# A recurrence's half-array products ordered head by head or in turn, and a slab begun on half its tokens

## What is computed

```python
# recurrence, per head
S_t = S_{t-1} diag(w_t) - (S_{t-1} kk_t)(kk_t*a_t)^T + v_t k_t^T ; y_t = S_t r_t
# the two borders
x = x + _rms_norm(mixed, norm_mix_post[i])
h = _rms_norm(x, norm_ffn_pre[i])                       # first border, then h @ w_ffn_up
f = jnp.square(jax.nn.relu(h @ w_ffn_up[i])) @ w_ffn_down[i]
x = x + _rms_norm(f, norm_ffn_post[i])
h = rmsnorm(x, norm_mix_g[l])                           # second border, then h @ w_in
```

## Time and profile before

| | us |
|---|---|
| median of three runs | 1532.68 (1531.84 to 1535.1) |
| the profiled execution | 1532.59 |
| its span, first to last instruction | 1530.8 |
| TensorE matmul busy | 1437.6 (94%) |
| VectorE busy | 736.2 (48%) |
| ScalarE busy | 613.0 (40%) |
| GpSimd busy | 473.7 (31%) |

### The profile page before, as it was taken

How to read it: one execution, slowest core, us unless ns; L and a number is a source line. 1 busy time by engine, 2 the same in 40 slices (tenths; PEclk the granted TensorE clock), 3 DMA queues, 4 the chain that set the end, 5 groups by cost and what they waited for, 6 DMA issues and landing times.

```text
span 1530.8 us, 19427 instructions
## 1 busy us (share of the span) xinstructions
PE 1437.6 (94%) x7762; PEld 1146.2 (75%) x7762; DVE 736.2 (48%) x1176; ACT 613.0 (40%) x960; POOL 473.7 (31%) x172
## 2 busy tenths in 40 slices
PE   6999999899889999999997999999999989699997
PEld 5878877688667888888886888777887867577763
DVE  3355367733354541514215199336353245566664
ACT  4443345322352432323214234654434444365552
POOL 2452023000124664645532454422233520200001
PEclk9999999657898999999998999999999999799998
DMA  6232123000134444444443234211223602889964
GB/s 215 90 117 70 32 88 110 2 1 1 42 138 132 157 136 153 140 149 143 146 150 111 83 108 126 83 55 35 105 83 137 214 11 103 341 333 422 412 270 180
DMA packets 98815, 207.61 MB, mean 136 GB/s; under 512 B 6785, under 2 KB 56321, under 8 KB 92065
## 3 DMA queue, kind: packets, MB, share of 16 engines
q1 hardware_dynamic: 91808, 181.13, 34.5%
q10 hardware_dynamic: 4608, 16.78, 2.8%
q0 software_dynamic: 2304, 8.39, 1.5%
HBM read 170.63 MB, written 35.65 MB: 135 GB/s over the span
## 4 chain that ended last, share of the span: by engine, by line
PE 82%; DVE 6%; ACT 5%; issue 3%; DMA 3%; POOL 1%; SPq 0%; POOLq 0%; DVEq 0%; ACTq 0%
PE bank L517 22%; PE bank L499 13%; PE bank L501 13%; PE bank L500 12%; PE bank L2876 4%; PE bank L809 3%; PE bank L785 3%; PE bank L800 2%; PE bank L1206 2%; ACT whi L428 1%; PE bank L706 1%; PE bank L2813 1%; PE bank L1160 1%; PE bank L1265 1%; PE bank L1280 1%
## 5 line engine op out<-in xcount | busy, mean ns | idle before, releaser
L436 POOL TENSOR_TENSOR wlo<-raw,whi 128x2048 fp32r<-128x2048 f32 (+2 forms) x83 | 378.7, 4562 | 652.7 <-ACT whi L428 616.4
L428 ACT ACTIVATE whi<-raw 128x2048 fp32r<-128x2048 f32 (+1 forms) x84 | 159.1, 1894 | 274.7 <-PE bank L501 267.4
L517 PE MATMUL bank<-alo,whi 128*128 128x512 f32 x368 | 149.2, 406 | 5.0 <-DVE alo L728 5.0
L2005 DVE TENSOR_TENSOR ffn_relu<-ffn_relu 128x512 f32<-128x512 f32 x32 | 97.6, 3051 | 106.7 <-ACT ffn_relu L1985 106.7
L517 PE MATMUL bank<-ahi,whi 128*128 128x512 f32 x368 | 146.5, 398 | 0.0
L499 PE MATMUL bank<-alo,whi 128*128 128x512 f32 (+1 forms) x360 | 141.5, 393 | 0.0
L501 PE MATMUL bank<-ahi,wlo 128*128 128x512 f32 (+1 forms) x360 | 140.3, 390 | 0.0
L500 PE MATMUL bank<-ahi,whi 128*128 128x512 f32 (+1 forms) x360 | 140.1, 389 | 0.0
L517 PE MATMUL bank<-ahi,wlo 128*128 128x512 f32 x368 | 91.7, 391 | 0.0
L517 PEld LDWEIGHTS bank<-alo,whi 128*128 128x128 f32 x368 | 71.3, 194 | 23.5 <-DVE alo L728 6.2
L517 PEld LDWEIGHTS bank<-ahi,whi 128*128 128x128 f32 x368 | 71.2, 193 | 15.5 <-issue 0.7
(11 more groups left out here) (517 smaller groups left out, 2994.0 us busy)
## 6 DMA issues: line engine op xcount, KB each, us to landing
raw<-in_w_in_dram SPq DMA_DIRECT2D x18, 1024.0 KB, 5.3
expert_gate_up<-in_expert_w_gate_dram SPq DMA_DIRECT2D x17, 1024.0 KB, 11.2
expert_gate_up<-in_expert_w_up_dram SPq DMA_DIRECT2D x17, 1024.0 KB, 13.9
expert_down<-in_expert_w_down_dram SPq DMA_DIRECT2D x17, 1024.0 KB, 8.7
raw<-in_w_ffn_up_dram SPq DMA_DIRECT2D x16, 1024.0 KB, 6.2
raw<-in_w_ffn_down_dram SPq DMA_DIRECT2D x16, 1024.0 KB, 5.6
raw<-in_w_in_first_dram SPq DMA_DIRECT2D x12, 1024.0 KB, 5.3
expert_rows_dram<-zero_rows SPq DMA_DIRECT2D x23, 512.0 KB, 6.9
```

Source lines behind the costliest of these rows:

```text
L428: nc.scalar.activation(whi[:, n % SPLIT, 0:k * c], raw[:, n % RAW, 0:k * c], ACT.Copy).then_inc(hi_made, 1)
L436: nc.gpsimd.tensor_tensor(wlo[:, n % SPLIT, 0:k * c], raw[:, n % RAW, 0:k * c], whi[:, n % SPLIT, 0:k * c].bitcast(F32), ALU.subtract).the ...
L517: ins = nc.tensor.matmul(acc, of, by, start=first and i == 0, stop=last and i == products - 1)
L2005: nc.vector.tensor_tensor(relu2[:, n % 2, :], relu[:, n % 2, :], relu[:, n % 2, :], ALU.mult).then_inc(up_sq, 1)
```

## The change

In the recurrence, the products of the two heads alternate in the masks, q, g, h and y. A mask stage now fills one bank for each head at the same time, and VectorE stores the masks in the new order. At both borders the function `pe_wide_early` does the first slab's 32 products with `whi` on the first 256 tokens before the last tiles are there: those of the first unit after the third turn, those of the second after the fourth. The 32 products on the last 256 tokens and the 16 with `wlo` on all 512 follow behind `columns_ready`. At the second border, ScalarE's and VectorE's lists have the second tile's split earlier.

```diff
+        def pe_wide_early(pe, name, turned):
...
+            for unit, cs in units:
+                pe.wait_ge(hi_made, n + 1)
+                pe.wait_ge(cols_lo, turns[turned]["split"] + NT // 2 * turns[turned]["halves"])
+                accs[unit] = banks.open(pe, unit)
+                for i in range(k):
+                    nc.tensor.matmul(accs[unit][:, near], wh[:, i, cs], alo[:, i, near], start=i == 0, stop=False, skip_group_check=True)
+                    nc.tensor.matmul(accs[unit][:, near], wh[:, i, cs], ahi[:, i, near], start=False, stop=False, skip_group_check=True)
+                yield
+            columns_ready(pe, turned)
+            for unit, cs in units:
+                for i in range(k):
+                    for acts in (alo, ahi):
+                        nc.tensor.matmul(accs[unit][:, far], wh[:, i, cs], acts[:, i, far], start=False, stop=False, skip_group_check=True)
+            pe.wait_ge(lo_made, n + 1)
+            for unit, cs in units:
+                for i in range(k):
+                    ins = nc.tensor.matmul(accs[unit][:, :], wl[:, i, cs], ahi[:, i, :], start=False, stop=i == k - 1, skip_group_check=True)
+                banks.filled(ins, unit)
+            yield
...
-            in_turn(turn)
+            in_order("turn early turn early early", turn=turn, early=early)
...
+            in_halves = [(NCH * h + c, h, c) for c in range(NCH) for h in range(2)]
...
-            for i, (src, h, c) in enumerate((src, h, c) for src in (b.beta, b.khat) for h in range(2) for c in (0, 2)):
-                acc = banks.open(pe, f"{u}mask{i}")
+            for i, (src, c) in enumerate((src, c) for src in (b.beta, b.khat) for c in (0, 2)):
+                names = [f"{u}mask{2 * i + h}" for h in range(2)]
+                accs = [banks.open(pe, name) for name in names]
                 for j in range(2):
...
+                    for h in range(2):
+                        ins = nc.tensor.matmul(accs[h][:, j * 256:(j + 1) * 256], src[half(h), (c + j) * CHUNK:(c + j + 1) * CHUNK],
+                                               b.kr[half(h), c + j, :, :].rearrange("p a n -> p (a n)"), start=True, stop=True)
...
-            for n, (h, c) in enumerate(units):
+            for n, h, c in in_halves:
...
+            for c in range(NCH):
+                cs = slice(c * CHUNK, (c + 1) * CHUNK)
+                for h in range(2):
+                    nc.tensor.matmul(yacc[half(h), cs], b.neg_w[:, NCH * h + c, 0:HD], b.ab[:, 1, NCH * h + c, :], start=c == 0, stop=False,
+                                     skip_group_check=True)
+                for h in range(2):
+                    nc.tensor.matmul(yacc[half(h), cs], b.vtok[:, c, half(h)], b.bd[:, 1, NCH * h + c, :], start=False, stop=True,
+                                     skip_group_check=True)
...
-            in_order("post norm post norm split post norm post slab norm split split split",
+            in_order("post norm post norm split post split norm post slab norm split split",
                      post=act_fed(act), norm=act_norm(act, "mix2", lambda t: x[:, t, :], x_ready_after(2), scratch3, sums3),
...
-            in_order("out gained post out gained norm post norm out gained post out gained norm post split norm split split split",
+            in_order("out gained post out gained norm post norm out gained post out gained norm post split split norm split split",
                      out=dve_last_down(dve), gained=dve_fed(dve), post=dve_post(dve, 1), split=dve_split(dve, "mix2", ahi, alo),
...
-            columns_ready(pe, "mix2")
-            for n in ("glu_gate0", "glu_gate1", "glu_a0", "glu_a1", "fq0", "fq1", "fk0", "fk1"):
+            for n in ("glu_gate1", "glu_a0", "glu_a1", "fq0", "fq1", "fk0", "fk1"):
```

More of the change, by code:

```diff
@@ L586, in pe_rows_open, with pe_rows_close @@
                 yield
-        def pe_rows_close(pe, names, units, turn, **how):
+        def pe_wide_early(pe, name, turned):
+            n = slab_no[name]
+            k, c = slab_shape(n)
+            wh, wl = view(whi, n % SPLIT, k, c), view(wlo, n % SPLIT, k, c)
+            near, far = slice(0, T // 2), slice(T // 2, T)
+            units = [(f"{name}/{j}", slice(j * P, (j + 1) * P)) for j in range(c // P)]
+            accs = {}
+            for unit, cs in units:
[17 more added lines that the diff above has]
+            yield
+        def pe_rows_close(pe, names, units, turn, early, **how):
             for t, hf in ((0, 0), (1, 0), (0, 1), (1, 1), (2, 0), (2, 1), (3, 0), (3, 1)):
@@ L1202, in pe_rwkv @@
             st.after("pool", "r")
-            for i, (src, h, c) in enumerate((src, h, c) for src in (b.beta, b.khat) for h in range(2) for c in (0, 2)):
-                acc = banks.open(pe, f"{u}mask{i}")
+            for i, (src, c) in enumerate((src, c) for src in (b.beta, b.khat) for c in (0, 2)):
+                names = [f"{u}mask{2 * i + h}" for h in range(2)]
+                accs = [banks.open(pe, name) for name in names]
                 for j in range(2):
[L1206 to L1210, removed]
+                    for h in range(2):
+                        ins = nc.tensor.matmul(accs[h][:, j * 256:(j + 1) * 256], src[half(h), (c + j) * CHUNK:(c + j + 1) * CHUNK],
+                                               b.kr[half(h), c + j, :, :].rearrange("p a n -> p (a n)"), start=True, stop=True)
+                        if j:
+                            banks.filled(ins, names[h])
+                yield
             st.after("act", "vtok")
@@ L1637, in dve_rwkv @@
                 acc = banks.take(dve, f"{u}mask{i}")
-                to = (b.ab, b.bd)[i // 4][:, :, 2 * (i % 4):2 * (i % 4) + 2, :].rearrange("p a c n -> p c a n")
+                first = NCH * (i % 2) + 2 * (i % 4 // 2)
+                to = (b.ab, b.bd)[i // 4][:, :, first:first + 2, :].rearrange("p a c n -> p c a n")
                 st.done(tt(to, acc[:, :].rearrange("p (c a n) -> p c a n", c=2, a=2),
@@ L1892, in pe_phase2 @@
             wait_pairs(pe)
-            pe_rows_close(pe, ["out.0.1", "out.1.1"], ["mix.0", "mix.1"], pe_turn(pe, "ffn", normal2_of))
-            columns_ready(pe, "ffn")
+            pe_rows_close(pe, ["out.0.1", "out.1.1"], ["mix.0", "mix.1"], pe_turn(pe, "ffn", normal2_of), pe_wide_early(pe, "up.0.0", "ffn"))
             for up, down in FFN_ORDER:
                 if up is not None:
-                    for s in range(4):
+                    for s in range(up == 0, 4):
                         pe_wide(pe, f"up.{up}.{s}")
@@ L1908, in pe_phase2 @@
                     pe_rows_close(pe, ["down.3.0.1", "down.3.1.1"], ["down.3.0", "down.3.1"],
-                                  pe_turn(pe, "mix2", normal3_of), acts=acts)
+                                  pe_turn(pe, "mix2", normal3_of), pe_wide_early(pe, "glu_gate0", "mix2"), acts=acts)
         def fed(eng, t):
```

17 lines of the change are left out of this document (8 added, 9 removed).

## The result

The changed kernel takes 1515.86 us, the median of four runs from 1509.31 to 1519.03, against 1533.42 for four runs of the kernel before: 17.6 us less. The recorded ratio, which is not that of these two medians, is 0.9876 with a 95% interval from 0.9854 to 0.9897 (the two medians alone give 0.9885). The forecast was 1512 in a range of 1503 to 1520. Both facts matter: in this execution every term of the sum came out within 1.3 us, 22.8 us in all for the 20.6 of the forecast, and the median is 6.5 us above it.

What follows compares the result with a forecast made beforehand. TensorE, 82% of the chain, was taken as the bound, with VectorE pacing the changed masks. Terms 3.2 + 4.3 + 3.5 + 3.4 + 4.0 + 2.2 = 20.6 us gave a forecast of 1512 us, range 1503 to 1520.

Steps and rivals of the forecast that it cites:

- Masks, pairs 0 and 1: Mask stages of pairs 0 and 1: alternating heads let VectorE set the pace; gain 3.2 us, bounds 0 and 5.4.
- Masks, pairs 2 and 3: Mask stages with attention steps, pairs 2 and 3: 18.3 us instead of 22.64; gain 4.3, between 0 and 5.4.
- the fourth rival: Pairs 2 and 3: the clock falls earlier, in the mask stages, 12 us lost there; 1539 in all, chance 0.04.
- the prediction's own sign: Whole kernel: the forecast is wrong if half-clock time moves by more than some 10 us either way.
- q, g, h, y: Output products: alternating heads overlap; gain 3.5 us in pairs 0 and 1, 3.0 (h, y) and 0.4 (q, g) in the last two.
- rival (1): q to y: alternating column halves do not run at once and gain nothing; 1519, chance 0.08.
- First border: First border's slab: early products use TensorE's gap and the clock returns earlier; gain 4.0 us, cases 2.6 to 5.6.
- Second border: Second border's slab: ends earlier though the last turn is held; gain 2.2 us, from a loss of 0.2 to 3.4.
- (2): Mask stages: masks stay at VectorE's present pace, so both mask gains, 7.5 us, are gone; 1519.5, chance 0.08.
- (3): Half-clock stretch of 73.2 us, pairs 2 and 3: breaks halfway, near 1494, or never falls, 1482; chance 0.07.

Runs made afterwards that it cites:

- The 1497.94: Changed kernel with mask-stage waits filled, plus constant products in the waits of pairs 2 and 3 around and behind the inversion: 1497.94 us, ratio 0.9783.

## Why the prediction was right, and where it was not

**Masks, pairs 0 and 1.** Forecast 3.2, and the profiled execution has 3.45. VectorE sets the pace as the four in the earlier trace rows said (0.61 a mask for their 0.63), and its last mask ends at 131.74, forecast 131.8. TensorE's inversion stretch then stays 11.10, so the gain went through. One link was otherwise: `bv` is held at its start, by pair 0's last mask (130.54, and `bv` starts at 130.64), and not in its second half, which starts at 132.45, 0.7 behind the last mask of all.

**Masks, pairs 2 and 3.** Forecast 4.3, measured 3.14. The term was mis-sized by the waits at the hand-over: VectorE is busy for 15.22 of 19.48 us and TensorE for 17.38. The 1 us added for them was 2.1, and what ends that wait is ScalarE's attention step behind its gathering copies, an engine that the sum left out.

**The step that failed** stands in the fourth rival: that the clock falls in the mask stages for the price of 12 us, all or nothing, at a chance of 0.04, with "Against: TensorE would be busy over 80% here". The busy share was right (17.38 of 19.48, and 13.24 of 15.13), and the clock falls all the same in some executions, behind the new waits of 1.89 and 2.1 us, for 4.8 and 4.9 us a place. By the prediction's own sign (the half-clock time moves by more than some 10 us) the first profile agrees with it, 85.3 us before and after, and the second does not: 102.4. So both mask terms, 7.5 us of the 20.6, are in the median worth about nothing (1.0008 alone; 0.9892 without them for 0.9876 and 0.99 with them). It is the rival's mechanism in a milder form, frequent where I had it rare. That the falls make up the 6.5 us from the shortest execution to the median is argued from five profiled falls and from the mean clocks, not shown for every execution, and with the two waits filled the median stayed. What brought 1515.86 within 4 us of 1512 is partly luck: the terms other than the masks gave 3.1 us more than forecast in the first profile and hid part of the loss. The range held it because it reached to the rivals in which the masks or the columns gain nothing.

**q, g, h, y.** Forecast 3.5 (7.4 us), measured 3.66 (7.26); forecast 3.0 (5.0 us), measured 3.03. Each at 0.055 a row, below the measured 0.0625 from eight rows. For q to h, 0.4 was forecast and 1.07 read, but the kernels with nothing changed there give 7.47 to 8.31, and those with the change 6.46 to 7.79: it depends on when the clock comes back. The rival (1) has fallen by the run of the columns alone. With it, the rule of the Trainium skill ("TensorE: Matmul & The Clock Gate", Part 3), that a weight load overlaps a running product only in another row group, is not borne out as the prediction applied it, to say that q to y would gain nothing: all rows of y use the same 128 rows of the array, and they start 0.055 apart in turn for 0.109 by head. The Trainium skill's "TensorEngine Tiling (Array Packing)", Key Properties, has it that different tiles load and multiply in parallel, and with that the trace agrees.

**First border.** Forecast 4.0 (2.6 to 5.6), measured 4.93. The gap took the first unit's products as said (16 at 0.12 apart), the second unit's ran at half clock, and the clock came back at about 451, in the far halves, earlier than before, as forecast; the reason given for it was not tested. The slab ends at 458.4, 8.5 us behind the last split: forecast 8 to 11.

**Second border.** Forecast 2.2 (-0.2 to 3.4), measured 3.49, a little past the end. The last turn starts 19.43 us behind the first for 16.57, so it was held by 2.9 us as forecast (3.3); but the clock was back at 809.5 us, ahead of the last turn, and the last part starts at 812.65 at full clock. I had it back at 829.6 in the time of before, which is behind the turn.

**Rivals (2) and (3).** (2), masks at VectorE's old pace, has fallen: twelve of them took 7.27 us. (3), that the half-clock stretch breaks, did not happen by the change, for the reason given: its waits belong to VectorE's inversion. Its price, 1482 with all of the half clock gone, was not met by filling the waits: the stretch kept the full clock, but of the 36 us only 14.7 came back, since the constants take some 18 and 4 are left as waits. The 1497.94 also has the masks' waits filled.

## What to carry over

A wait of 2 us that faster products open on TensorE can cost more than the work it saved, by the clock of what follows; before counting such a gain, ask what work can move into the new wait. Compare stages between the same instructions of several executions, not medians alone: here gains of 3 us in a stage are sharp to 0.1 us, where the clock is the same, while medians of a few runs move by 3. And where a long stretch runs at half clock with all its products back to back, look at the short waits ahead of it and in it: with products that compute nothing in all of them 14.7 us came back, with those ahead of it alone 4.1 (69.54 for 73.65), and in the profile of the kernel before 2.4, since the clock fell there all the same.

## What was not expected

The same instructions with the same wait (2.10 and 2.11 us) kept the clock in one execution and lost it in another, and a wait of 0.5 us was followed by a fall in one kernel and not in its neighbour. Waits that look alike in the profile are a chance of a fall, not a fall. The times spread widely: 15.2 us over twelve executions with the masks alone, and 9.7 over four of the changed kernel. But the first border alone, with the old masks, spreads over 10.9 in twelve, and the second over 9.6, so the new waits are not the only source of it. The kernel before is steadier, but less so than its first four runs (3.3 us) said: 29 more, beside the parts alone, spread over 8.1, from 1530.61 to 1538.73.
